# Sample keys and values swept in pairs into different output row groups, with the sample token blocks beside them

## What is computed

```python
def _dilated_gather_sample(q, kv_new, kv_buf, bias_tab, window, dil):
    kv_all = jnp.concatenate([kv_buf, kv_new], axis=1)
    jj = np.arange(window // dil + 1)
    idx = lb + np.arange(t)[:, None] - jj[None, :] * dil
    g = kv_all[:, np.maximum(idx, 0)]
    logits = jnp.einsum('bthd,btkhd->bthk', q, g[:, :, :, 0]) * SCALE + bias
    ...
    p = jnp.exp(logits - lse[..., None])
    o = jnp.einsum('bthk,btkhd->bthd', p, g[:, :, :, 1])
```

## Time and profile before

| | us |
|---|---|
| median of 3 runs | 1918.89 |
| lowest of them | 1915.81 |
| the profiled execution, its own time | 1915.16 |
| its span, first to last instruction | 1913.4 |
| TensorE busy | 1632.7 (85%) |
| VectorE busy | 1104.6 (58%) |
| ScalarE busy | 591.8 (31%) |
| POOL busy | 683.2 (36%) |
| DMA moved | 729.73 MB, mean 381 GB/s |

### The profile page before, as it was taken

The page is one execution under the profiler, slowest core; times in us unless marked ns, Lnnn a source line. Parts: engine busy times, 40 slices in busy tenths (PEclk is TensorE's granted clock), DMA queues, the critical chain, the costliest instruction groups (busy, mean ns, idle before and its releaser), DMA issues.

```text
span 1913.4 us, 18474 instructions
## 1 busy us (share of the span) xinstructions
PE 1632.7 (85%) x5880; PEld 887.8 (46%) x5880; DVE 1104.6 (58%) x2752; ACT 591.8 (31%) x1850; POOL 683.2 (36%) x672
## 2 busy tenths in 40 slices
PE   6999989998888878777789999998987877877776
PEld 4777954454343333222147887554543323322321
DVE  2331485766877874444423317747777777744444
ACT  2141233333334332222332313323333333322222
POOL 2130144445443444333312102444544444433331
PEclk9899999999998899999999999999999998899999
DMA  6797699999999999999958796999999999999996
GB/s 198 289 371 271 254 404 421 421 421 421 421 421 421 421 422 421 422 421 421 422 222 334 277 341 255 405 421 421 421 421 422 421 421 421 422 421 421 422 422 261
DMA packets 102488, 729.73 MB, mean 381 GB/s; under 512 B 14827, under 2 KB 15925, under 8 KB 21624
## 3 DMA queue, kind: packets, MB, share of 16 engines
q0 software_dynamic: 90112, 627.43, 79.5%
q1 hardware_dynamic: 11732, 100.48, 13.7%
q10 hardware_dynamic: 548, 0.65, 0.1%
HBM read 724.25 MB, written 48.10 MB: 404 GB/s over the span
## 4 chain that ended last, share of the span: by engine, by line
DMA 44%; PE 39%; DVE 10%; ACT 2%; issue 2%; DVEq 2%; POOL 1%; ACTq 1%; SPq 0%; POOLq 0%
DMA arena<-peer_uv,idx 26%; PE bank L1603 15%; DMA wring<-peer_uv,idx 7%; PE bank L1385 6%; DMA qf<-peer_uv,idx 6%; DMA yt<-peer_uv,idx 4%; PE bank L1569 3%; PE bank L1380 3%; DVE arena L1233 3%; PE bank L1539 3%; PE bank L1448 1%; PE bank L1418 1%; DVE wring L1233 1%; ACT diag L809 1%; DVE route L1205 1%
## 5 line engine op out<-in xcount | busy, mean ns | idle before, releaser
L1603 PE MATMUL bank<-arena,diag 128*128 128x512 f32 (+1 forms) x1464 | 701.7, 623 | 159.2 <-ACT diag L809 159.1
L609 POOL DMA_INDIRECT arena<-peer_uv,idx x366 | 400.7, 1095 | 670.1 <-PE bank L1603 487.4
L1233 DVE SCALAR_TENSOR_TENSOR arena<-arena,xn 128x1024 f32<-128x1024 f32 x366 | 443.1, 1224 | 294.8 <-DMA arena<-peer_uv,idx 293.1
L1603 PEld LDWEIGHTS bank<-arena,diag 128*128 128x128 f32 (+1 forms) x1464 | 266.7, 189 | 552.1 <-issue 307.4
L801 ACT ACTIVATE act<-hid 128x2 f32<-128x2 f32 x288 | 58.6, 203 | 913.4 <-DVE arena L1233 597.1
L1603 PE MATMUL bank<-wring,diag 128*128 128x512 f32 (+1 forms) x384 | 187.5, 611 | 41.1 <-ACT diag L809 40.9
L809 ACT ACTIVATE diag<-ident,weight 128x128 f32<-128x128 f32 (+1 forms) x576 | 194.7, 385 | 21.0 <-issue 1.4
L1233 DVE SCALAR_TENSOR_TENSOR wring<-wring,xn 128x1024 f32<-128x1024 f32 x96 | 117.5, 1224 | 80.3 <-DMA wring<-peer_uv,idx 79.2
L609 POOL DMA_INDIRECT wring<-peer_uv,idx x96 | 101.5, 1057 | 149.2 <-PE bank L1603 145.5
L1603 PE MATMUL bank<-qf,diag 128*128 128x512 f32 (+1 forms) x248 | 122.5, 633 | 32.5 <-ACT diag L809 32.5
L804 ACT ACTIVATE weight<-act,gate 128x1 f32<-128x1 f32 x576 | 138.2, 287 | 20.1 <-issue 0.3
(11 more groups left out here) (254 smaller groups left out, 1516.7 us busy)
## 6 DMA issues: line engine op xcount, KB each, us to landing
kvs<-cache_a_kv_w SPq DMA_DIRECT2D x32, 1022.0 KB, 9.1
wring<-w_col SPq DMA_DIRECT2D x16, 1024.0 KB, 6.4
wring<-w_tok SPq DMA_DIRECT2D x8, 1408.0 KB, 10.5
arena<-peer_wq SPq DMA_DIRECT2D x10, 1024.0 KB, 13.8
kvs<-cache_a_kv_w SPq DMA_DIRECT2D x16, 508.0 KB, 7.8
arena<-peer_uv,idx POOLq DMA_INDIRECT x366, 21.9
qf<-cache_keys POOLq DMA_DIRECT2D x10, 576.0 KB, 7.3
qf<-cache_values POOLq DMA_DIRECT2D x8, 576.0 KB, 8.7
```

Of the source, the lines that this page charges most:

```text
L609: pool.indirect_dma_start(out=ring[j], out_offset=None, in_=io["peer_uv"], in_offset=bass.IndirectOffsetOnAxis(ap=idx[:, n:n + 1], axis=0) ...
L1233: last = v.scalar_tensor_tensor(out=ring[j][:, 0:D], in0=ring[j][:, 0:D], scalar=1.0, in1=xn[:, i, :], op0=ALU.mult, op1=ALU.mult, accum_o ...
L1603: last = pe.matmul(bank[b0 + half][0:r, :], diag[:, n % 16, 0:r], ring[SLOT_OF[n]][:, D + 512 * half:D + 512 * half + 512], start=False, s ...
```

## The change

Samples are taken in pairs, one of each row group: keys as (0, 4), (1, 5), (2, 6), (3, 7), values as (1, 5), (2, 6) and then (0, 4), (3, 7). Within a pair the matmuls alternate between the two samples, block by block. AS moves to rows 64 to 95 and BS to rows 96 to 127 of their banks; behind every second block of a pair stands one matmul of AS (pairs 0 and 1) or BS (pairs 2 and 3). `out` therefore takes a range of the contraction. The one `qk_mean` stands between pairs 0 and 1. POOL loads keys and values in the new order. `pv_done` counts both last matmuls of the values. `values` alternates between even and odd heads.

```diff
--- before.py
+++ after.py
@@ -76,6 +76,9 @@
 COPY_AFTER = (None, None, 4, 21, 33, 43, 44, 45, 46, 56)
 SCORE_AFTER = {2: 3, 3: 20, 4: 32, 5: 40, 9: 41}
 COPY_LAG = 2
+KEY_ORDER = (0, 4, 1, 5, 2, 6, 3, 7)
+VALUE_ORDER = ((1, 5), (2, 6), (0, 4), (3, 7))
+S_ROWS = {"AS": slice(2 * NS, 3 * NS), "BS": slice(3 * NS, 4 * NS)}
 
 FIRST, REST, WHOLE = slice(0, P), slice(P, TOKENS), slice(0, TOKENS)
 Q_ORDER = [(1, 0, FIRST), (1, 1, FIRST), (2, 0, FIRST), (2, 1, FIRST), (0, 0, REST), (0, 1, REST)]
@@ -479,7 +482,7 @@
                     load_w(l, c)
                     for m in range(3 * (c - 2) // 2, 3 * (c - 1) // 2 if c < N_IN else 17):
                         shift(l, m)
-                sp.wait_ge(pv_done, l + 1)
+                sp.wait_ge(pv_done, 2 * (l + 1))
                 load_o(l, 1)
                 for m in range(17, 19):
                     shift(l, m)
@@ -543,7 +546,7 @@
                 else:
 
                     pool.wait_ge(bias_sample, 1)
-                for b in range(NB - 1):
+                for b in KEY_ORDER[0:NB - 1]:
                     load_k(l, b)
                 if l:
                     pool.wait_ge(xs_ps, 6 * l)
@@ -561,9 +564,9 @@
                 load_k(l, NB - 1)
                 pool.wait_ge(qk_done, 6 * (l + 1))
                 pool.memset(pz, 0.0).then_inc(pz_clear, 1)
-                for b in range(1, NB - 1):
-                    pool.wait_ge(key_ps, NB * l + b + 1)
-                    load_v(l, b)
+                for n in range(1, NB - 1):
+                    pool.wait_ge(key_ps, NB * l + n + 1)
+                    load_v(l, KEY_ORDER[n])
                 pool.wait_ge(key_ps, NB * (l + 1))
                 load_v(l, 0)
                 load_v(l, NB - 1)
@@ -661,14 +664,14 @@
             def tok_out(l, name):
 
                 i = 2 if name[1] == "S" else int(name[1])
-                r, b = ROWS[i], out_bank(name)
+                r, b = ROWS[i], out_bank(name)[S_ROWS[name] if i == 2 else slice(0, P), :]
                 vals = kvn[:, 1, :] if i == 2 else tok[:, i, 0:AW]
                 a.wait_ge(in_ps, len(OUTS) * l + OUTS.index(name) + 1)
                 if name[0] == "A":
-                    a.activation(vals[0:r, 0:TOK_W], b[0:r, 0:TOK_W], ACT.Copy).then_inc(took_a, 1)
+                    a.activation(vals[0:r, 0:TOK_W], b[:, 0:TOK_W], ACT.Copy).then_inc(took_a, 1)
                 else:
-                    a.activation(vals[0:r, TOK_W:AW], b[0:r, 0:AW - TOK_W], ACT.Copy)
-                    a.activation(tok[0:r, i, AW:TOK], b[0:r, AW - TOK_W:TOK_W], ACT.Gelu_apprx_tanh).then_inc(took_a, 1)
+                    a.activation(vals[0:r, TOK_W:AW], b[:, 0:AW - TOK_W], ACT.Copy)
+                    a.activation(tok[0:r, i, AW:TOK], b[:, AW - TOK_W:TOK_W], ACT.Gelu_apprx_tanh).then_inc(took_a, 1)
 
             def cv_squares(l, tiles):
 
@@ -731,7 +734,7 @@
 
             def sample_value_copy(l):
 
-                a.wait_ge(pv_done, l + 1)
+                a.wait_ge(pv_done, 2 * (l + 1))
                 a.activation(pvs[0:2 * NS, :, :], pv_ps, ACT.Copy).then_inc(pv_copied, 1)
 
             def sample_value_out(l):
@@ -1367,23 +1370,26 @@
                     if old in BY_DVE:
                         pe.wait_ge(took_d, by_dve(l, old))
 
-            def out(l, name):
+            def out(l, name, ks=range(KCH)):
 
                 c = CHUNK_OF[name]
-                pe.wait_ge(w_loaded[c % 2], w_target(l, c))
-                bank_free(l, name)
+                if 0 in ks:
+                    pe.wait_ge(w_loaded[c % 2], w_target(l, c))
+                    bank_free(l, name)
                 b = out_bank(name)
                 if name[0] in "AB":
                     i = 2 if name[1] == "S" else int(name[1])
                     w = wring[:, c % 2, 0:KCH * TOK_W].rearrange("p (k n) -> p k n", k=KCH)
-                    for k in range(KCH):
-                        last = pe.matmul(b[0:ROWS[i], 0:TOK_W], xt[:, k, cols_of(i)], w[:, k, :], start=(k == 0), stop=(k == KCH - 1))
+                    r = S_ROWS[name] if i == 2 else slice(0, P)
+                    for k in ks:
+                        last = pe.matmul(b[r, 0:TOK_W], xt[:, k, cols_of(i)], w[:, k, :], start=(k == 0), stop=(k == KCH - 1))
                 else:
                     j = CHUNKS[c][1].index(name)
                     w = wring[:, c % 2, 0:KCH * PAIR].rearrange("p (k n) -> p k n", k=KCH)
-                    for k in range(KCH):
+                    for k in ks:
                         last = pe.matmul(b[:, 0:TOKENS], w[:, k, j * P:(j + 1) * P], xt[:, k, :], start=(k == 0), stop=(k == KCH - 1))
-                last.then_inc(in_ps, 1)
+                if KCH - 1 in ks:
+                    last.then_inc(in_ps, 1)
 
             def qk_mean(l, j):
 
@@ -1406,17 +1412,25 @@
                 far = [[far_windows(buf)[:, g, a, NS * (NT * b4 + t):NS * (NT * b4 + t) + NS] for t in range(NT)] for g in range(2)]
                 return slice(NS * a, NS * a + NS), near, far
 
-            def sample_keys(l, b):
-
-                if b == 0:
+            def sample_keys(l, n, between=()):
+
+                pair = KEY_ORDER[2 * n:2 * n + 2]
+                if n == 0:
                     pe.wait_ge(qz_done, l + 1)
-                pe.wait_ge(k_in[b], 16 * (l + 1))
-                r, near, far = windows_of(qz, b)
-                pe.matmul(slog[r, 0, 0:P], near, kc[b][:, 8, :], start=(b % 4 == 0), stop=False)
-                for t in range(NT):
-                    for g in range(2):
-                        last = pe.matmul(slog[r, g + 1, 0:P], far[g][t], kc[b][:, 4 * g + t, :], start=False, stop=False)
-                last.then_inc(key_ps, 1)
+                for b in pair:
+                    pe.wait_ge(k_in[b], 16 * (l + 1))
+                for c in range(9):
+                    for b in pair:
+                        r, near, far = windows_of(qz, b)
+                        if c == 0:
+                            last = pe.matmul(slog[r, 0, 0:P], near, kc[b][:, 8, :], start=(n == 0), stop=False)
+                        else:
+                            t, g = (c - 1) // 2, (c - 1) % 2
+                            last = pe.matmul(slog[r, g + 1, 0:P], far[g][t], kc[b][:, 4 * g + t, :], start=False, stop=False)
+                        if c == 8:
+                            last.then_inc(key_ps, 1)
+                    if c % 2 and c // 2 < len(between):
+                        out(l, *between[c // 2])
 
             def new_logits(l):
 
@@ -1438,16 +1452,21 @@
                 for g in range(NG):
                     pe.matmul(pv_ps[:, g, :], ptn[0:NS, g, :], kvn[:, 1, g * P:(g + 1) * P], start=(g == 0), stop=False)
 
-            def sample_values(l, b):
-
-                pe.wait_ge(v_in[b], 16 * (l + 1))
-                r, near, far = windows_of(pz, b)
-                pe.matmul(pv_ps[r, 0, :], near, vc[b][:, 8, :], start=False, stop=False)
-                for t in range(NT):
-                    for g in range(2):
-                        last = pe.matmul(pv_ps[r, g + 1, :], far[g][t], vc[b][:, 4 * g + t, :], start=False, stop=(b in (0, NB - 1) and t == NT - 1 and g == 1))
-                if b == NB - 1:
-                    last.then_inc(pv_done, 1)
+            def sample_values(l, pair):
+
+                for b in pair:
+                    pe.wait_ge(v_in[b], 16 * (l + 1))
+                for c in range(9):
+                    for b in pair:
+                        r, near, far = windows_of(pz, b)
+                        if c == 0:
+                            pe.matmul(pv_ps[r, 0, :], near, vc[b][:, 8, :], start=False, stop=False)
+                        else:
+                            t, g = (c - 1) // 2, (c - 1) % 2
+                            end = pair == VALUE_ORDER[-1] and c == 8
+                            last = pe.matmul(pv_ps[r, g + 1, :], far[g][t], vc[b][:, 4 * g + t, :], start=False, stop=end)
+                            if end:
+                                last.then_inc(pv_done, 1)
 
             def turn_sample_values(l):
 
@@ -1483,9 +1502,9 @@
             def values(l, slot, q):
 
                 pe.wait_ge(probt_done, 3 * l + slot + 1)
-                for h in range(HEADS):
-                    r = slice(64 * (h % 2), 64 * (h % 2) + 64)
-                    for kb in range(q + 1):
+                for g, kb, side in [(g, kb, side) for g in range(NG) for kb in range(q + 1) for side in range(2)]:
+                        h = 2 * g + side
+                        r = slice(64 * (h % 2), 64 * (h % 2) + 64)
                         j = h * (q + 1) + kb
                         last = pe.matmul(ya_bank[q][r, (h // 2) * P:(h // 2 + 1) * P], tok[:, kb, h * HD:h * HD + HD],
                                          (pt0 if q == 0 else pt1)[:, j, :], start=(kb == 0), stop=(kb == q))
@@ -1635,15 +1654,11 @@
                 out(l, "k2")
                 qk_mean(l, 3)
                 qk_mean(l, 4)
-                for b in range(0, 3):
```

(19 more changed lines are left out.)

## The result

| | before, us | after, us |
|---|---|---|
| median | 1917.4 (4 runs) | 1894.31 (4 runs, 1893.27 to 1901.29) |
| the profiled execution, its own time | 1915.16 | 1901.29 |
| its span | 1913.4 | 1899.6 |
| TensorE busy | 1632.7 | 1606.5 |

The ratio is 0.9887 with a 95% interval of 0.987 to 0.9904. One of the four runs of before took 5499.3 us; it counts in the median of 1917.4 but not in the ratio, for which the other three have a median of 1915.91. So 21.6 us were gained, where the sum of the forecast had 30. The profiled execution of after is its slowest, 7 us above its median, so part of what its trace shows is its own; what the second trace shows too belongs to the kernel.

The account below looks back on a forecast made before the run. TensorE was taken to set the pace. Gains of 12.4 us in layer 0 and 17.6 in layer 1, together 30, took 1915.16 to 1885.2, plus one: 1886 us; own range 1880 to 1892, over the cases 1877 to 1900.

Parts of the forecast that it names:

- each row group goes at its own spacing and the busiest one sets the time: TensorE, keys and values: matmuls in different row groups overlap, key passes 0.109 us apart, AS and BS passes about 0.30.
- the 11.4 of the sum: Keys with AS, BS and one qk_mean, without any wait: 11.4 us in place of 24.14, at least 10.3.
- 2.85 from empty: Keys: time in us of a pair that starts on an empty array; some 2.5 behind another pair.
- that rival (1967): Keys and values: each switch of row group costs a drain, no overlap, 52 us slower; chance 0.02.
- the one without overlap: Keys and values: nothing overlaps that didn't before, time stays at 1916; chance 0.02.
- The values: Sample values in pairs, 4 x 1.96 = 7.85 in place of 14.73: gain 6.9 us a layer.
- The loads of layer 0: Keys, layer 0: late loads leave 5.5 of 12.7 us gain, bounds 4.2 to 6.5; samples 3 and 7 there at 103.7.
- The half clock: TensorE in the new gaps: a granted clock of half would add to the sum; not costed.
- Layer 1: Keys, layer 1: only sample 7's load is close; gain 10.7 us, bounds 9 to 12.7.
- What is late next: Behind the keys: probabilities behind BS, xb1's weights (bounds 0 to 3 us a layer) and value loads, each costed at 0.
- All of the gain arrives: Rival, both layers: full 19.6 us a layer, 39 in all, giving 1877; chance 0.08.
- The transfers take the keys' gain: Rival: TensorE waits for late weights at xb1, T1 or u1, keys' gain partly or wholly lost, 1896 to 1902; chance 0.15.

Follow-up runs that it names:

- spread_own: Changed kernel with cache copies moved away from the keys and output projection's weights, and an own buffer for sample 7's keys: 1878.74 against 1918.78, again 1876.83 against 1914.67.
- one_after_other: spread_own with the two samples of a pair one behind the other, AS or BS still between: 1886.59 against 1915.49, a single execution.
- after_again: The changed kernel, unaltered, in a second set of runs with a second trace: 1891.76 against 1914.67, ratio 0.9868.
- hold_chunk7: Changed kernel with SP's weight chunk 7 (xb0) and the copies behind it held until six samples' keys are used: 1892.13 against 1918.78, a single execution.
- own_buffer: Changed kernel with a buffer of its own for sample 7's keys, loaded right behind the other seven: 1893.06 against 1913.51, ratio 0.9891.
- keys_only: Changed kernel with the values part put back as before, only keys, AS and BS and all loads in the new order: 1906.7 against 1913.51, ratio 0.9964.
- before_spread: Kernel before, with cache copies moved away from the keys, seven of them last behind the query weights: 1916.73 against 1918.78, ratio 0.9993.
- copies_later: Changed kernel with cache copies around the sample keys moved behind the last weight chunks, buffers as in the change: 1899.24 against 1913.51, ratio 0.9928.

## Why the prediction was right and where it was wrong

The time, 1894.31, lies inside the range of 1877 to 1900 and on the side forecast, and 8 us above the forecast itself; it lies outside the forecast's own range of 1880 to 1892, which the second median (1891.76) just meets. The 1 us that the prediction added for the other runs had no ground: its median of 1918.89 counted the run of 5499.3, and without it the runs of before give 1915.9.

**The overlap: right.** The step "each row group goes at its own spacing and the busiest one sets the time" holds: 0.11 and 0.30 between starts, in the same microseconds. Without loads in the way the keys take 10.1, nearer to the floor of 10.3 than to the 11.4 of the sum; they fall 0.2 below that floor because a pass of AS is nearer to 0.295 than to 0.30. The pair "2.85 from empty" took 2.74, and in spread_own the rest goes at the pace of AS and BS, as said for the floor. The rule of strict program order in the Trainium skill, "TensorE: Matmul & The Clock Gate" (section "The mechanism"), was weighed against the trace, and one_after_other contradicts it in its first row above: a pass of another row group starts ahead of earlier ones, if of a few only. Alternating costs no drain, so that rival (1967) falls, and so does the one without overlap.

**The values: right.** 6.63 a layer for 6.9; a half takes 4.05 instead of 3.92. L1490 gained 0.05.

**The loads of layer 0: the mechanism was right, the term was mis-sized.** The sum had samples 3 and 7 there at 103.7, bounds 102.7 and 105. That is 15.8 us behind the first pair, and 14.8 to 17.1 by its bounds; after has 20.2, after_again 19.7. The step that failed is "a sample's 0.59 MB takes 6.1 us at the one rate and 3.8 at the other, so the bounds are 102.7 and 105": it added the difference of the two rates, 2.4 us, to the landing of before. But that landing ("issued at 90.39 with 12.3 to landing") was a price from a stretch in which SP's queue was running dry: sample 7 came at 102.7, only 1.4 us behind the load ahead of it (101.3). In after SP's next chunk is issued at 95.9 and keeps its queue full; sample 3 came at 104.15 and sample 7 5.75 us behind it, at 109.9. These 5.75 in place of 1.4 are, but for rounding, the 4.4 that were missing; the 1 us that the forecast did add went into sample 3 (14.3 behind the first pass, 13.4 before). The landing of a load has to be taken from the one ahead of it in its queue, at the rate of that stretch: 101.3 and the prediction's own 6.1 give 107.4, 19.5 behind the first pass, where 20.2 and 19.7 were measured. hold_chunk7 shows the cause (sample 7 again 1.4 us behind sample 3, 101.8 and 100.4), own_buffer excludes the late issue.

**The half clock: known and left out.** "A granted clock of half in the new gaps isn't in the sum and would add to it" came true: the last pair at 1.2 GHz took 4.76 in place of 2.85, 1.9 us. It is in the last pair of layer 0 in both traces of after, and in that of layer 1 in the first. Together with the 4.4 this is the 6.3 by which layer 0's keys missed the forecast (24.94 against 18.7), so that layer 0 has no gain in its keys at all.

**Layer 1: right, in one of the two traces of after and in keys_only.** after_again's 13.83 and keys_only's 14.19 stand to the forecast of 13.4 (1037.1 less 1023.65), with the wait for cache_keys in the forecast 1 to 3 us (2.05 and 2.29). In the profiled execution of after the wait was 3.59 and the clock fell, 18.33: 4.9 us more. A wait of 0.9 to 1.5 for w_tok was there besides, which the prediction didn't have. Why this one load came later that time isn't known.

**What is late next: right, at 0.** The probabilities behind BS stay hidden: 35.31 from keys to values. They are ready 0.5 us before TensorE takes them (VectorE's last operation ends at 123.15, the transposes start at 123.66), which is little cover; spread_own, with earlier keys, still has 35.31. For xb1's weights no wait shows: from the keys' end to the values TensorE has no gap in either trace of after. What is over 35.31 there (0.48 in layer 1 of after, 0.41 in layer 0 of after_again) is the half clock of the last pair, which lasts 1 us into what follows.

**The rivals.** *All of the gain arrives* (1877) asked for no wait, and after has three; it is what spread_own does (1878.74 and 1876.83, gains of 40.0 and 37.8 us against the 39 of that rival), once the copies and the buffer are out of the way. *The transfers take the keys' gain* (1896 to 1902) named the place wrongly: it looked for the weights behind the keys, in front of xb1, T1 or u1, but what it would take in layer 0 was taken, by key loads that come late inside the keys. In layer 1 it wasn't. The result of 1894 lies between the forecast and this rival, and so does what happened.

**The accounts.** From the profiled execution of before to the one of after, in us: start of the keys in layer 0 +1.9 (nothing of the change lies ahead of it; after_again has -0.8 there), keys of layer 0 +0.8, of layer 1 -5.8, values -13.3 together, all the rest +2.5 (1.9 of it between layer 0's output projection and layer 1's keys). But for rounding their sum is -13.8, which is 1899.6 less 1913.4.

## What to carry to other kernels

When TensorE's work is shortened in a stretch where the DMA engines are full, forecast each load's landing from the one ahead of it in its queue and from what the other queue has issued by then: what TensorE frees earlier is also issued earlier, and it slows the very loads that are now wanted sooner. Look for traffic that nobody waits for (here the copies of the cache) and move it to a stretch in which the DMA share is low before counting the gain, because the move shows nothing as long as TensorE is the bound (before_spread 0.9993) and some 10 us once it isn't. Work for different row groups of TensorE has to alternate matmul by matmul in the program; with one block behind the other a third to nearly a half of the keys' gain is lost (14.6 and 16.3 us against 10.1, from 24.14).

## What the runs showed of the hardware that was not expected

- **The run-ahead between row groups is short.** In one_after_other a pass of another row group started ahead of three earlier passes of a 128-column stream (91.52 against 91.62 to 91.84), and no further.
- **The queues got packets in equal number.** With both backlogged, 236 packets each in 10 us carried 3.13 MB for SP's and 0.96 MB for POOL's; alone POOL's moved 0.94 MB in 4 us (hold_chunk7). It was the queue with the smaller packets that came off worse.
- **A wait on a load can cost twice.** After waits of 3.59 to 6.33 us ahead of the last pair (after, after_again in layer 0, keys_only, own_buffer) the pair ran at the half level, with passes 0.21 and 0.59 us apart in place of 0.11 and 0.30, and lost about 2 us; after 2.05 and 2.29 us it ran at full clock. The length of the last wait doesn't settle it: in copies_later the clock fell (0.50 from 105.0 to 108.3) behind a wait of 2.08 us, and in after it fell inside the third pair, behind 2.59 and 1.31. Which of these falls and which doesn't was only observed, not set by an experiment.
